# Second feed-forward: first convolution tap on ScalarE, gate product and low half moved one step later

## Chip, cores and metric

The kernel runs on one core of a Trainium2 chip. The metric is the device time of one execution in microseconds. Everything is fp32. The run shown is one profiled execution; the time quoted is a median over unprofiled runs.

## The reference

Two transformer blocks with two layers each run one after the other on an activation of 256 tokens by 1024. The change touches only the feed-forward of the second block, which is computed once in each of its two layers:

```
h = rmsnorm(x, norm_ffn_g[l])
u = centred_depthwise_conv(h @ w_up[l], ffn_conv_w[l])   # w_up: 1024 x 5632, three taps along the tokens
u_gate, u_val = jnp.split(u, 2, axis=-1)                 # 2816 columns each
x = x + (jax.nn.silu(u_gate) * u_val) @ w_down[l]        # w_down: 2816 x 1024
```

`silu(v)` is `v * sigmoid(v)`. The convolution multiplies each column (a feature) at tokens t-1, t and t+1 by three weights of that column and adds.

## The kernel before

**Products in three passes.** Every fp32 matrix product is made of three matmuls (`mm3`, L682 to L684) over operands that are split into a high half (rounded to the type fp32r) and a low half (the rest): high x high, high x low, low x high. Weights come from memory in units of 128 x 2048 numbers into `raw` (5 buffers). ScalarE writes the high half `whi` (L1231), VectorE subtracts it for the low half `wlo` (L1610); both have 3 buffers, so ScalarE's split of unit u waits until TensorE is through with unit u-3. Activations are split in the same way: `high` on ScalarE (key `hiT`), `low` on VectorE (L1617).

**One written order.** `Plan` writes one list of steps. Every engine walks through the same list and issues its own part of each step, in this order: `step` first issues the weight splits up to two units ahead of the step (`ahead`), and then the step's own work (`do`). An engine runs its instructions strictly in this order. A split of weights that stands behind another instruction on its engine thus waits for it.

**The stage.** `ffn2(l)` first runs a normalisation (`rms`) and `fstart` (clears the two border columns of `ci`, loads the convolution weights `cwf`). Then come the up products `("up", l, cb, k)`: column blocks cb = 0 to 5, of 512 columns each (256 in block 5), k = 0 for the gate half and k = 1 for the value half. The result of one has the features on the partitions: 4 chunks of 128 features x 256 tokens (2 in block 5). A full one uses two units of weights, one in block 5 a single unit. Behind them come the down products `("dn", l, 0)` and `("dn", l, 1)`, of six units each, unit j of which needs chunk group j of `hT2`, the hidden activation. So units 0 to 21 are the up weights, and 22 on the down weights; these numbers within the stage are used below. At the last unit of an up product (cb, k), each engine does in `product`:

- ScalarE: the eviction from PSUM to `ci[k]` (L1464), then `convolved` for the product before: for k = 0 the sigmoid of `co[0]` into `sgf` (L1474), which waits for the taps; for k = 1 the high half `hT2h` (L1477), which waits for the last product `co[0] * co[1]` (key `fm`).
- VectorE: `convolve` for the product before: tap 0 (L2421, `co[k] = ci[k] * w0`, one instruction for each chunk), taps 1 and 2 (L2423, multiply and add), and then for k = 0 the gate product `co[0] *= sgf` (L2427), which waits for the sigmoid; for k = 1 `co[1] = co[0] * co[1]` (L2430) and `low` into `hT2l` (L1617), which waits for `hT2h`.

A "turn" is what VectorE does from one `convolve` to the next. The turn of k = 1 or k = 0 is named after the half that it convolves. After the product (5, 1) the order goes on with the first unit of the down product, `fend` (`convolve` and `convolved` of (5, 1)), and the other down units.

Of the kernel before, what the change touches and what calls it, by code (L numbers as in the profile page):

```python
# [12 lines left out]
ACT = mybir.ActivationFunctionType  # L13
# [8 lines left out]
ALL = slice(None)  # L22
# [224 lines left out]
class Plan:  # L247
# [219 lines left out]
    def ffn2(self, l):  # L467
        a, m, o = self.a, self.m, self.order
        o += [("rms", f"f2{l}"), ("fstart", l)]
        xt = [("xT", f"f2{l}", 1)]  # L470
        for cb in range(6):
            for k in range(2):
                o += self.gemm(("up", l, cb, k), "ffn2", m.xT, a["w_up_2"][l], "b", 8, 2816 * k + 512 * cb,
                               min(512, 2816 - 512 * cb), xt)
        need = [("hT2", l, c) for c in range(6)]
        dn = [self.gemm(("dn", l, cb), "ffn2", m.hT2, a["w_down_2"][l], "a", 22, 512 * cb, 512, need) for cb in range(2)]
        o += dn[0][0:1] + [("fend", l)] + dn[0][1:] + dn[1]
        if l == 1:
            o += [("out", "out")]

# [741 lines left out]
class Scalar(Engine):  # L1222
# [157 lines left out]
    def product(self, g, G):  # L1380

        e, m, nm = self.e, self.m, g[0]
        if nm in ("bo", "bd", "wo", "w2", "w3", "e3", "oat", "od", "wo2", "dn"):
            if nm == "w3":
                cb, n = g[1], G.w // 128
                e.wait_ge(*self.at("ev", "w3", cb))
                e.activation(m.hT[0][:, 4 * cb:4 * cb + n, :],
                             m.tmp[:, 0:2 * G.w].rearrange("p (k n) -> p k n", n=256), ACT.Copy) \
                    .then_inc(*self.up("hi_ffn", ("hiT", "hT", cb)))
            return  # L1390
        ps = self.psum(*g)
        if nm == "g":
            return
        e.wait_ge(*self.at("full", *g))
        if nm in ("q", "k"):
            dst = m.qT if nm == "q" else m.kT
            e.activation(dst[:, 4 * g[2]:4 * g[2] + 4, :], bands(ps, 4), ACT.Copy).then_inc(*self.up("a_qkv", ("ev",) + g))
        elif nm == "v":
            e.activation(m.v[:, :, 512 * g[2]:512 * g[2] + 512], bands(ps), ACT.Copy) \
                .then_inc(*self.up("a_qkv", ("ev",) + g))  # L1400
        elif nm in ("cq", "ck"):
            dst = m.cq if nm == "cq" else m.ck
            e.activation(dst[:, :, :], bands(ps)[:, :, 0:G.w], ACT.Copy).then_inc(*self.up("a_latent", ("ev",) + g))
        elif nm == "uq":
            e.activation(m.qr[:, :, G.n0:G.n0 + G.w], bands(ps)[:, :, 0:G.w], ACT.Copy) \
                .then_inc(*self.up("a_latent", ("ev",) + g))
        elif nm == "ukv":
            cb = g[2]
            for t in range(2):
                pv = ps[:, t * 512:t * 512 + 512].rearrange("p (h n) -> p h n", h=4)  # L1410
                e.activation(m.kk[:, t, 4 * cb:4 * cb + 4, 0:64], pv[:, :, 0:64], ACT.Copy)
                ins = e.activation(m.vm[:, t, 4 * cb:4 * cb + 4, :], pv[:, :, 64:128], ACT.Copy)
            ins.then_inc(*self.up("a_latent", ("ev",) + g))
        elif nm == "w1":
            if g[1]:
                e.wait_ge(*self.at("ev", "w3", g[1] - 1))
            e.activation(m.sgm[:, 0:2 * G.w], ps[:, 0:2 * G.w], ACT.Sigmoid).then_inc(*self.up("a_ffn", ("sgm", g[1])))
        elif nm == "pp":
            gP = m.gP if g[1] == 0 else m.gP1
            e.activation(gP[:, g[2]], bands(ps), ACT.Copy).then_inc(*self.up("a_ple", ("ev",) + g))  # L1420
        elif nm == "pg":
            if g[2]:
                e.wait_ge(*self.at("py", g[1], 0))
            gE = m.gE if g[1] == 0 else m.gE1
            e.activation(gE[:, :, :], bands(ps), ACT.Sigmoid).then_inc(*self.up("a_ple", ("ev",) + g))
        elif nm == "rt":
            e.activation(m.lgt[:, :, :], bands(ps)[:, :, 0:8], ACT.Copy).then_inc(*self.up("a_route", ("ev",) + g))
        elif nm == "e1":
            ex, cb = g[1:]
            if cb > 1:  # L1430
                e.wait_ge(*self.at("full", "ac", ex, cb - 2))
            elif ex:
                e.wait_ge(*self.at("full", "sc", ex - 1, cb))
            e.activation(m.hb[:, cb % 2, 0:self.tiles, :], bands(ps)[:, 0:self.tiles, :], ACT.Sigmoid) \
                .then_inc(*self.up("a_moe", ("hbs", ex, cb)))
        elif nm == "e2":
            e.activation(m.hb[:, g[2], 0:self.tiles, :], bands(ps)[:, 0:self.tiles, :], ACT.Copy) \
                .then_inc(*self.up("a_moe", ("ev",) + g))
        elif nm == "dc":
            if g[2] == 2:  # L1440
                e.wait_ge(*self.at("tap", g[1], 0))
            e.activation(m.cin[g[2] % 2][:, :, 2:258], bands(ps, 4), ACT.Copy).then_inc(*self.up("a_conv", ("ev",) + g))
        elif nm == "z":
            zr = m.odn[:, :, :, :].rearrange("p t h n -> p t (h n)")
            for r, t, y in ROWS:
                ins = e.activation(zr[r, y, :], bands(ps)[r, t, :], ACT.Copy)
            ins.then_inc(*self.up("a_conv", ("ev",) + g))
        elif nm == "bd2":
            self.beta(g, ps)
        elif nm == "gm":  # L1450
            e.activation(m.gm[:, (g[2] + 2) % 4], bands(ps), ACT.Sigmoid).then_inc(*self.up("a_gate2", ("ev",) + g))
        elif nm == "qa":
            e.activation(m.qk[:, :, 0:8, :], ps[:, :].rearrange("p (t h n) -> p t h n", t=2, n=64), ACT.Copy) \
                .then_inc(*self.up("a_grid", ("ev",) + g))
        elif nm == "ka":
            pv = ps[:, :].rearrange("p (t h n) -> p t h n", t=2, n=64)
            e.activation(m.qk[:, :, 8:10, :], pv[:, :, 0:2, :], ACT.Copy)
            e.activation(m.va[:, :, :, :], pv[:, :, 2:4, :], ACT.Copy).then_inc(*self.up("a_grid", ("ev",) + g))
        elif nm == "up":
            _, l, cb, k = g  # L1460
            n = G.w // 128
            if cb:
                e.wait_ge(*self.at("ftap", l, cb - 1, k))
            e.activation(m.ci[k][:, 0:n, 1:257], ps[:, 0:2 * G.w].rearrange("p (c n) -> p c n", c=n), ACT.Copy) \  # L1464
                .then_inc(*self.up("a_ffn2", ("ev",) + g))
            if (cb, k) != (0, 0):
                self.convolved(l, cb - 1 + k, 1 - k)

    def convolved(self, l, cb, k):
        e, m = self.e, self.m  # L1470
# [132 lines left out]
class Vector(Engine):  # L1603
# [26 lines left out]
    def do(self, step):  # L1630
# [149 lines left out]
        elif what == "fstart":  # L1780
            for k in range(2):
                e.memset(m.ci[k][:, :, 0:1], 0.0)
                ins = e.memset(m.ci[k][:, :, 257:258], 0.0)
            ins.then_inc(*self.up("d_ffn2"))
        elif what == "fend":
            self.convolve(a[0], 5, 1)

    def tables(self):

# [245 lines left out]
    def product(self, g, G):  # L2035
# [6 lines left out]
        ps = self.psum(*g)  # L2042
        if nm == "up":
            _, l, cb, k = g
            if (cb, k) != (0, 0):
                self.convolve(l, cb - 1 + k, 1 - k)
            return
# [357 lines left out]
        e.tensor_tensor(of, of, m.zs[:, :, :], ALU.mult).then_inc(*self.up("d_delta", ("odn", l)))  # L2405

    def convolve(self, l, cb, k):
        e, m = self.e, self.m
        n = min(512, 2816 - 512 * cb) // 128
        co, ci = m.co[k], m.ci[k]  # L2410
        if (cb, k) == (0, 0):
            e.wait_ge(*self.at("ld", "cwf", l))
        e.wait_ge(*self.at("ev", "up", l, cb, k))
        if cb:
            e.wait_ge(*self.at("hiT", "hT2", l, cb - 1))
        for tap in range(3):
            e.wait_ge(*self.prev)
            for c in range(n):
                wc = m.cwf[:, 22 * k + 4 * cb + c, tap:tap + 1]
                if tap == 0:  # L2420
                    ins = e.tensor_scalar(co[:, c, :], ci[:, c, 0:256], wc, None, ALU.mult)  # L2421
                else:
                    ins = e.scalar_tensor_tensor(co[:, c, :], ci[:, c, tap:tap + 256], wc, co[:, c, :], ALU.mult, ALU.add)  # L2423
            ins.then_inc(*self.up("d_ffn2", ("ftap", l, cb, k)))
        if k == 0:
            e.wait_ge(*self.at("fsg", l, cb))
            e.tensor_tensor(co[:, 0:n, :], co[:, 0:n, :], m.sgf[:, 0:n, :], ALU.mult).then_inc(*self.up("d_ffn2"))  # L2427
        else:
            e.wait_ge(*self.prev)
            e.tensor_tensor(co[:, 0:n, :], m.co[0][:, 0:n, :], co[:, 0:n, :], ALU.mult) \  # L2430
                .then_inc(*self.up("d_ffn2", ("fm", l, cb)))
            self.low("ffn2", ("hT2", l, cb), co[:, 0:n, :], m.hT2, (ALL, slice(4 * cb, 4 * cb + n), ALL))


class Pool(Engine):
# [299 lines left out]
```

## Time and profile before

| | |
|---|---|
| median of 3 runs | 3000.89 us (2997.72 to 3003.07) |
| the profiled execution | 3003.25 us |
| its span, first to last instruction | 3001.4 us |
| mean granted TensorE clock | 0.967 of full speed |
| TensorE matmul busy | 2781.7 us, 93% of the span |
| VectorE busy | 2140.1 us, 71% |
| ScalarE busy | 1597.6 us, 53% |
| GpSimd busy | 141.8 us, 5% |

Busy shares are over the whole span. The stage in question runs twice, from about 2276 to 2489 us and from about 2789 us to the end. Matmuls are pipelined, so that TensorE counts as busy for longer than a matmul holds up the next.

### The profile page before, as it was taken

To read this page: it belongs to the slowest core of one execution; us is meant where nothing else is said; L and a number is where in the kernel's file an instruction comes from. 1 tells how busy PE (TensorE), PEld (TensorE's weight loads), DVE (VectorE), ACT (ScalarE), POOL (GpSimd) and SP (SyncE) were. 2 spreads that over 40 slices of the span, in tenths; PEclk is the share of its full clock that TensorE was granted. 3 is DMA by queue.
4 is the path that set the end of the run, shared out by engine and by line. 5 is a ranking of instruction groups with operands and counts; after the bars stand their busy time and mean duration, and the time that the engine had idled before them with its cause. 6 is when DMAs were issued, how large, how long until landed. Compare 5 with 4: busy or idle time off the path is not lost.

```text
span 3001.4 us, 44783 instructions
## 1 busy us (share of the span) xinstructions
PE 2781.7 (93%) x19184; PEld 2363.0 (79%) x19184; DVE 2140.1 (71%) x2148; ACT 1597.6 (53%) x1532; POOL 141.8 (5%) x154
## 2 busy tenths in 40 slices
PE   7988999998889999999999999979989989988998
PEld 7867799886777787878778787768778978877896
DVE  4557655646659897988889898867755866766685
ACT  3345443354437676767667676736544434654442
POOL 0000000000000000000000000000420000051000
PEclk9899999999989999999999999989999999999999
DMA  5253555455348898999989999953214544312452
GB/s 182 96 153 133 179 177 182 134 169 145 117 150 311 317 354 318 342 327 346 326 316 343 329 353 334 350 166 114 72 66 142 169 166 151 124 59 93 142 169 98
DMA packets 360206, 616.16 MB, mean 205 GB/s; under 512 B 13760, under 2 KB 117056, under 8 KB 359984
## 3 DMA queue, kind: packets, MB, share of 16 engines
q1 hardware_dynamic: 354784, 597.50, 57.6%
q0 software_dynamic: 5200, 15.47, 2.1%
q8 instruction: 168, 2.75, 0.4%
q14 instruction: 54, 0.44, 0.0%
HBM read 611.88 MB, written 1.05 MB: 204 GB/s over the span
## 4 chain that ended last, share of the span: by engine, by line
PE 74%; DVE 15%; ACT 6%; issue 4%; DMA 1%; POOL 0%; ACTq 0%; DVEq 0%; SPq 0%; POOLq 0%
PE ps L682 21%; PE ps L684 21%; PE ps L683 21%; DVE wlo L1610 4%; ACT whi L1231 3%; DVE co L2423 2%; PE ps L914 1%; PE ps L945 1%; PE ps L1091 1%; PE ps L935 1%; DVE cv L2240 1%; PE ps L1070 1%; DVE co L2421 1%; PE ps L775 1%; PE ps L1102 1%
## 5 line engine op out<-in xcount | busy, mean ns | idle before, releaser
L1610 DVE TENSOR_TENSOR wlo<-raw,whi 128x2048 fp32r<-128x2048 f32 (+2 forms) x588 | 1303.5, 2223 | 460.3 <-ACT whi L1231 455.9
L1231 ACT ACTIVATE whi<-raw 128x2048 fp32r<-128x2048 f32 (+2 forms) x588 | 1090.6, 1859 | 463.3 <-PE ps L684 450.6
L682 PE MATMUL ps<-whi,xTh 128*128 128x512 f32 (+5 forms) x1488 | 599.8, 403 | 30.3 <-issue 16.8
L683 PE MATMUL ps<-wlo,xTh 128*128 128x512 f32 (+5 forms) x1488 | 588.7, 396 | 0.0
L684 PE MATMUL ps<-whi,xTl 128*128 128x512 f32 (+5 forms) x1488 | 587.7, 395 | 0.0
L682 PE MATMUL ps<-xTh,whi 128*128 128x256 f32 x1504 | 428.8, 285 | 24.1 <-DVE xTl L1617 11.9
L684 PE MATMUL ps<-xTh,wlo 128*128 128x256 f32 x1504 | 427.2, 284 | 0.0
L683 PE MATMUL ps<-xTl,whi 128*128 128x256 f32 x1504 | 425.7, 283 | 0.0
L682 PEld LDWEIGHTS ps<-whi,xTh 128*128 128x128 f32 x1488 | 291.4, 196 | 96.6 <-issue 21.2
L684 PEld LDWEIGHTS ps<-whi,xTl 128*128 128x128 f32 x1488 | 291.8, 196 | 63.9
L683 PEld LDWEIGHTS ps<-wlo,xTh 128*128 128x128 f32 x1488 | 292.4, 196 | 58.7
L682 PEld LDWEIGHTS ps<-xTh,whi 128*128 128x128 f32 x1504 | 286.1, 190 | 27.8 <-issue 15.4
L683 PEld LDWEIGHTS ps<-xTl,whi 128*128 128x128 f32 x1504 | 286.9, 191 | 0.1
L684 PEld LDWEIGHTS ps<-xTh,wlo 128*128 128x128 f32 x1504 | 284.8, 189 | 0.0
L682 PE MATMUL ps<-whi,hTeh 128*128 128x512 f32 x448 | 178.3, 398 | 0.0
L683 PE MATMUL ps<-wlo,hTeh 128*128 128x512 f32 x448 | 177.6, 396 | 0.0
L684 PE MATMUL ps<-whi,hTel 128*128 128x512 f32 x448 | 177.6, 396 | 0.0
L684 PEld LDWEIGHTS ps<-whi,hTel 128*128 128x128 f32 x448 | 84.4, 188 | 20.6
L682 PEld LDWEIGHTS ps<-whi,hTeh 128*128 128x128 f32 x448 | 84.4, 188 | 20.2
L683 PEld LDWEIGHTS ps<-wlo,hTeh 128*128 128x128 f32 x448 | 84.4, 188 | 20.1
L682 PE MATMUL ps<-whi,hT2h 128*128 128x512 f32 x176 | 71.4, 406 | 14.7 <-DVE wlo L1610 14.4
L2423 DVE SCALAR_TENSOR_TENSOR co<-ci,cwf,co 128x256 f32<-128x256 f32 x176 | 74.0, 481 | 1.7
(533 smaller groups left out, 3450.2 us busy)
## 6 DMA issues: line engine op xcount, KB each, us to landing
raw<-in_expert_w_dram SPq DMA_DIRECT2D x336, 1024.0 KB, 6.0
raw<-in_w_in_dram SPq DMA_DIRECT2D x76, 1024.0 KB, 5.1
raw<-in_w_up_dram SPq DMA_DIRECT2D x44, 1024.0 KB, 5.3
raw<-in_dense_w_dram SPq DMA_DIRECT2D x32, 1024.0 KB, 5.1
raw<-in_w_down_dram SPq DMA_DIRECT2D x20, 1024.0 KB, 5.9
raw<-in_w_out_dram SPq DMA_DIRECT2D x16, 1024.0 KB, 5.1
raw<-in_w_branch_diff_dram SPq DMA_DIRECT2D x8, 1024.0 KB, 5.0
raw<-in_w_ple_gate_dram SPq DMA_DIRECT2D x8, 1024.0 KB, 5.1
```

The costliest lines, as they stand in the source:

```text
L682: self.e.matmul(out, ah, bh, start=start, stop=False)
L683: self.e.matmul(out, ah, bl, start=False, stop=False)
L684: return self.e.matmul(out, al, bh, start=False, stop=stop)
L775: ins = self.e.transpose(ps[:, k * 128:k * 128 + 128], src[:, t, k * 128:k * 128 + 128], self.m.ident[:, :])
L914: ins = e.matmul(ps[:, d * 256:d * 256 + 256], m.xs[half][:, q, (d0 + d) * 128:(d0 + d + 1) * 128], m.sel[:, q, :], start=(q == 0), stop=( ...
L935: ins = e.transpose(ps[:, o:o + 128], m.hb[:, cb % 2, t, k * 128:k * 128 + 128], m.ident[:, :])
L945: ins = e.matmul(ps[:, q * 512:q * 512 + 512], m.selgT[:, s, q * 128:q * 128 + 128], m.hb[:, cb, s, :], start=(s == 0), stop=(s == self.ti ...
L1070: ins = self.e.transpose(out(r_), src[:, 128 * r_:128 * r_ + 128], self.m.ident[:, :])
L1091: ins = e.matmul(ps[half(a_), span(512 * c + 64 * r_)], m.E[d][r, s], TT[r, s], start=True, stop=True)
L1231: self.e.activation(self.m.hi[u % NHL][:, 0:n], self.m.raw[u % NRAW][:, 0:n], ACT.Copy) \
L1610: self.e.tensor_tensor(self.m.lo[u % NHL][:, 0:n], self.m.raw[u % NRAW][:, 0:n], self.m.hi[u % NHL][:, 0:n].bitcast(F32), ALU.subtract) \
L2423: ins = e.scalar_tensor_tensor(co[:, c, :], ci[:, c, tap:tap + 256], wc, co[:, c, :], ALU.mult, ALU.add)
```

## The change

The first tap of the convolution moves from VectorE to ScalarE. There it stands in `product`, behind the eviction and behind `convolved`, as one activation (copy with a scale for each partition) for each chunk. It is tap 0 of the product just evicted, not of the product before. ScalarE waits there for its own eviction, for `cwf` and the cleared borders at the first product, and for `low` of the block before, where it writes `co[1]`.

On VectorE `convolve` keeps taps 1 and 2. The gate product moves from the end of the k = 0 turn to the k = 1 turn, behind its taps and ahead of the last product. The low half moves out of `convolve` into `hidden_low`, which runs at the start of the next k = 0 turn; for block 5 it is a step of its own, `flast`, behind the second down unit.

```diff
-        o += dn[0][0:1] + [("fend", l)] + dn[0][1:] + dn[1]
+        o += dn[0][0:1] + [("fend", l)] + dn[0][1:2] + [("flast", l)] + dn[0][2:] + dn[1]
...
             e.activation(m.ci[k][:, 0:n, 1:257], ps[:, 0:2 * G.w].rearrange("p (c n) -> p c n", c=n), ACT.Copy) \
                 .then_inc(*self.up("a_ffn2", ("ev",) + g))
-            if (cb, k) != (0, 0):
+            copied = self.prev
+            if (cb, k) == (0, 0):
+                e.wait_ge(*self.at("ld", "cwf", l))
+                e.wait_ge(*self.at("fzero", l))
+            else:
                 self.convolved(l, cb - 1 + k, 1 - k)
+            e.wait_ge(*copied)
+            if cb and k:
+                e.wait_ge(*self.at("hT2", l, cb - 1))
+            for c in range(n):
+                wc = m.cwf[:, 22 * k + 4 * cb + c, 0:1]
+                ins = e.activation(m.co[k][:, c, :], m.ci[k][:, c, 0:256], ACT.Copy, scale=wc)
+            ins.then_inc(*self.up("a_ffn2", ("tap0", l, cb, k)))
...
+        elif what == "flast":
+            self.hidden_low(a[0], 5)
...
             _, l, cb, k = g
+            if cb and k:
+                self.hidden_low(l, cb - 1)
             if (cb, k) != (0, 0):
                 self.convolve(l, cb - 1 + k, 1 - k)
...
-        e.wait_ge(*self.at("ev", "up", l, cb, k))
-        if cb:
-            e.wait_ge(*self.at("hiT", "hT2", l, cb - 1))
-        for tap in range(3):
-            e.wait_ge(*self.prev)
+        e.wait_ge(*self.at("tap0", l, cb, k))
+        for tap in (1, 2):
+            if tap == 2:
+                e.wait_ge(*self.prev)
             for c in range(n):
                 wc = m.cwf[:, 22 * k + 4 * cb + c, tap:tap + 1]
-                if tap == 0:
-                    ins = e.tensor_scalar(co[:, c, :], ci[:, c, 0:256], wc, None, ALU.mult)
-                else:
-                    ins = e.scalar_tensor_tensor(co[:, c, :], ci[:, c, tap:tap + 256], wc, co[:, c, :], ALU.mult, ALU.add)
+                ins = e.scalar_tensor_tensor(co[:, c, :], ci[:, c, tap:tap + 256], wc, co[:, c, :], ALU.mult, ALU.add)
             ins.then_inc(*self.up("d_ffn2", ("ftap", l, cb, k)))
-        if k == 0:
+        if k == 1:
+            done = self.prev
             e.wait_ge(*self.at("fsg", l, cb))
-            e.tensor_tensor(co[:, 0:n, :], co[:, 0:n, :], m.sgf[:, 0:n, :], ALU.mult).then_inc(*self.up("d_ffn2"))
-        else:
+            e.tensor_tensor(m.co[0][:, 0:n, :], m.co[0][:, 0:n, :], m.sgf[:, 0:n, :], ALU.mult).then_inc(*self.up("d_ffn2"))
+            e.wait_ge(*done)
             e.wait_ge(*self.prev)
             e.tensor_tensor(co[:, 0:n, :], m.co[0][:, 0:n, :], co[:, 0:n, :], ALU.mult) \
                 .then_inc(*self.up("d_ffn2", ("fm", l, cb)))
-            self.low("ffn2", ("hT2", l, cb), co[:, 0:n, :], m.hT2, (ALL, slice(4 * cb, 4 * cb + n), ALL))
+
+    def hidden_low(self, l, cb):
+        n = min(512, 2816 - 512 * cb) // 128
+        self.low("ffn2", ("hT2", l, cb), self.m.co[1][:, 0:n, :], self.m.hT2, (ALL, slice(4 * cb, 4 * cb + n), ALL))
```

## Rows read from the trace of the kernel before

**Rows 1.** The page, part 1: busy time of each engine, share of span

```profile
PE 2781.7 (93%) x19184; PEld 2363.0 (79%) x19184; DVE 2140.1 (71%) x2148; ACT 1597.6 (53%) x1532; POOL 141.8 (5%) x154
```

**Rows 2.** TensorE waits, 2270 to 2440 us: line, releaser, total, times, longest

```profile
PE ps L682 <- DVE wlo L1610: 8.6, 5, 5.1
```

**Rows 3.** The same view, 2785 to 3001 us, second layer

```profile
PE ps L682 <- DVE wlo L1610: 10.7, 6, 5.1
```

**Rows 4.** Busy time by stretch: length, engines (instructions), granted clock, DMA share, GB/s

```profile
2294.00:2341.22 47.22, 47.22 (x396) 47.22 (x395) 36.17 (x49) 24.09 (x17) 0.00 (x0) 1.00 0.51 161
...
2366.28:2391.34 25.06, 23.51 (x194) 23.16 (x194) 21.47 (x33) 11.27 (x8) 0.00 (x0) 1.00 0.50 165
```

**Rows 5.** VectorE in order of time: start, us, instruction, idle before it and releaser

```profile
2366.20 1.14 DVE L2421 TENSOR_SCALAR co<-ci,cwf 128x256 f32<-128x256 f32 x4
2367.37 3.38 DVE L2423 SCALAR_TENSOR_TENSOR co<-ci,cwf,co 128x256 f32<-128x256 f32 x8
2370.79 1.23 DVE L2430 TENSOR_TENSOR co<-co,co 128x1024 f32<-128x1024 f32 x1
2373.14 1.23 DVE L1617 TENSOR_TENSOR hT2l<-co,hT2h 128x1024 fp32r<-128x1024 f32 x1 [1.13 <-ACT hT2h L1477]
2374.94 4.50 DVE L1610 TENSOR_TENSOR wlo<-raw,whi 128x2048 fp32r<-128x2048 f32 x2 [0.58 <-ACT whi L1231]
2379.36 1.14 DVE L2421 TENSOR_SCALAR co<-ci,cwf 128x256 f32<-128x256 f32 x4
2380.53 3.38 DVE L2423 SCALAR_TENSOR_TENSOR co<-ci,cwf,co 128x256 f32<-128x256 f32 x8
2385.04 1.23 DVE L2427 TENSOR_TENSOR co<-co,sgf 128x1024 f32<-128x1024 f32 x1 [1.13 <-ACT sgf L1474]
2386.85 4.49 DVE L1610 TENSOR_TENSOR wlo<-raw,whi 128x2048 fp32r<-128x2048 f32 x2 [0.58 <-ACT whi L1231]
2391.26 1.14 DVE L2421 TENSOR_SCALAR co<-ci,cwf 128x256 f32<-128x256 f32 x4
```

**Rows 6.** ScalarE in the same stretch, in order of time

```profile
2372.05 1.06 ACT L1477 ACTIVATE hT2h<-co 128x1024 fp32r<-128x1024 f32 x1 [6.91 <-DVE co L2430]
2373.01 3.70 ACT L1231 ACTIVATE whi<-raw 128x2048 fp32r<-128x2048 f32 x2
2376.62 1.00 ACT L1464 ACTIVATE ci<-ps 128x1024 f32<-128x1024 f32 x1
2383.95 1.06 ACT L1474 ACTIVATE sgf<-co 128x1024 f32<-128x1024 f32 x1 [6.33 <-DVE co L2423]
2384.91 3.71 ACT L1231 ACTIVATE whi<-raw 128x2048 fp32r<-128x2048 f32 x2
```

**Rows 7.** ScalarE groups by shape: busy us, mean ns | idle before, releaser

```profile
L1504 ACT ACTIVATE sg__147<-sg__147,mxg 128x256 f32<-128x256 f32 x32 | 15.9, 499 | 17.2 <-DVE mxg L1909 17.2
```

**Rows 8.** VectorE at the start of the first layer's stage

```profile
2304.19 1.14 DVE L2421 TENSOR_SCALAR co<-ci,cwf 128x256 f32<-128x256 f32 x4
...
2311.67 4.49 DVE L1610 TENSOR_TENSOR wlo<-raw,whi 128x2048 fp32r<-128x2048 f32 x2 [0.58 <-ACT whi L1231]
```

**Rows 9.** ScalarE at the start of the first layer's stage

```profile
2306.77 1.28 ACT L1474 ACT_TABLE_LOAD   x1
2308.77 1.06 ACT L1474 ACTIVATE sgf<-co 128x1024 f32<-128x1024 f32 x1 [0.71 <-DVE co L2423]
```

**Rows 10.** VectorE's weight splits at the end of the first layer's stage

```profile
2411.91 2.29 DVE L1610 TENSOR_TENSOR wlo<-raw,whi 128x2048 fp32r<-128x2048 f32 x1 [0.58 <-ACT whi L1231]
...
2422.85 2.29 DVE L1610 TENSOR_TENSOR wlo<-raw,whi 128x2048 fp32r<-128x2048 f32 x1 [0.57 <-ACT whi L1231]
...
2430.00 2.29 DVE L1610 TENSOR_TENSOR wlo<-raw,whi 128x2048 fp32r<-128x2048 f32 x1 [1.11 <-ACT whi L1231]
...
2437.88 5.63 DVE L1610 TENSOR_TENSOR wlo<-raw,whi 128x2048 fp32r<-128x2048 f32 x3 [1.11 <-ACT whi L1231]
```

**Rows 11.** TensorE in a short stretch: busy time and granted clock

```profile
2426.00:2429.00 3.00, 3.00 (x9) 0.55 0.89 281
```

More of the change, by code:

```diff
@@ L1783, in do @@
                 ins = e.memset(m.ci[k][:, :, 257:258], 0.0)
-            ins.then_inc(*self.up("d_ffn2"))
+            ins.then_inc(*self.up("d_ffn2", ("fzero", a[0])))
         elif what == "fend":
             self.convolve(a[0], 5, 1)
+        elif what == "flast":
+            self.hidden_low(a[0], 5)
     def tables(self):
```

## The prediction

> **What bounds the kernel now.** I read the page first. TensorE is busy for 93% of the span, VectorE 71%, ScalarE 53% [rows 1]. An average over unlike stages says nothing of this one, so I went to TensorE's waits inside the stage: it waits for VectorE's split `wlo`, 8.6 us in 5 waits in the first layer and 10.7 us in 6 in the second [rows 2, 3]. So VectorE's side is the slower one, but not by much. The stretches show from when: from 2294 to 2341 us TensorE is busy throughout (47.22 of 47.22 us, 396 matmuls, so 0.119 us each), and a block of 192 matmuls would take it 22.9 us. From 2366.28 to 2391.34 us one block takes 25.06 us [rows 4]. The head start is used up by then, and about 2.2 us a block are lost.
>
> What makes 25.06 us is a loop through two engines, and VectorE's and ScalarE's timelines show it link by link [rows 5, 6]. I measure each link from start to start, as neighbours overlap a little.
>
> Turn k=1: tap 0 1.17 (2366.20 to 2367.37), taps 1 and 2 3.42, `co0*co1` 1.26 (2370.79 to ScalarE's 2372.05), `hT2h` 0.96, first `whi` 1.93, two `wlo` 4.42: 13.16 us. Turn k=0: tap 0 1.17, taps 3.42, sigmoid 0.96, `whi` 1.94, two `wlo` 4.41: 11.90 us. The two are 25.06 us.
>
> Two things do not appear in these sums: the gate product of turn k=0 (2385.04) and the low half of turn k=1 (2373.14). Both run while VectorE waits for ScalarE's `whi` anyway: of the 2.9 us between the last tap or product and the next `wlo`, VectorE idles 1.13 + 0.58 and works 1.23 at no cost. They are free today. And `whi` cannot come sooner, since in ScalarE's written order it stands behind `hT2h` or the sigmoid.
>
> **The change, part by part.**
>
> *Tap 0 leaves VectorE.* Saves 1.17 us in every turn, on the loop.
>
> *Tap 0 on ScalarE.* It stands behind the sigmoid or `hT2h` and ahead of the next `whi`, for which VectorE, and then TensorE, wait. ScalarE's idle 6.3 and 6.9 us [rows 6] lie before these instructions and are no cover: the order puts the taps behind them. So all of it is on the loop. No row has this form. The nearest is ScalarE's activation of 128x256 in SBUF with a bias for each partition, 0.50 us [rows 7]; neighbours overlap by 0.10 (`hT2h` takes 1.06 and the next starts after 0.96), so 0.40 each and 1.60 for four. From below: a plain copy takes 1.06 for 1024 columns and about 1.90 for 2048 [rows 6], so 0.43 for 256 by that line, 0.33 spaced, 1.32 for four. From above: 0.50 without overlap, 2.00. I take 0.40, because the scale is an operand for each partition as the bias in that row is.
>
> *Gate product into turn k=1.* It leaves the free place and comes between the taps and `co0*co1`, on which it bears: +1.26 in turn k=1, the spacing of such a product and what waits for it; 0 saved in turn k=0.
>
> *Low half into turn k=0.* It leaves the other free place and stands ahead of the taps: +1.15 (1.23 less the 0.08 by which neighbours overlap, as 4.50 against 4.42). Nothing saved in turn k=1.
>
> So turn k=1: 13.16 - 1.17 + 1.26 + 1.60 = 14.85, +1.69. Turn k=0: 11.90 - 1.17 + 1.15 + 1.60 = 13.48, +1.58. A block goes from 25.06 to 28.33 us, and VectorE's idle time in it from 3.6 to about 9 us. That is the point: VectorE gets less work and more waiting.
>
> *The waits.* The added ones (own eviction, `cwf`, the borders, `low` of the block before) are met long before, save the own eviction at the very first product, behind which ScalarE's split has slack. TensorE's buffers bring no new wait: two units need 11.5 us in a turn of 13.5.
>
> *The start.* The loop governs from the `wlo` at 2311.67 on [rows 8]. After the change two tap passes run from 2304.19 to 2307.61, but the sigmoid also waits for its table load, which ends at 2308.05 [rows 9]. From there 0.96 + 1.60 + 1.94 give 2312.6: +0.9.
>
> *Full turns.* From 2311.67 to 2411.91 [rows 8, 10] are 100.24 us, four blocks of 25.06. Added: 4 x (1.69 + 1.58) = 13.1.
>
> *The end.* Three shorter turns follow, to 2422.85, 2430.00 and 2437.88 [rows 10], where a tap 0 issued for block 5 has two chunks (0.80). Value half of block 4: -1.17 + 1.26 + 0.80 = +0.9. Gate half of block 5: -0.6 + 1.15 + 0.80 = +1.35. Value half of block 5, with nothing for ScalarE behind it: -0.6 + 0.7 = +0.1. `flast` stands behind the split at 2437.88, for which TensorE waits, and its result is wanted two units later: 0. SyncE's loads wait for `wlo` five units back and get more time; GpSimd's load of the next gains waits for `flast` and has until the next normalisation at about 2484.
>
> Per layer 0.9 + 13.1 + 2.35 = 16.35. Behind 2437.88 TensorE alone sets the time, so all of it reaches the end. The second layer has the same pattern and waits [rows 3]: in all 32.7 us. On the profiled execution's 3003.25 us that is 3036. This execution lies 2.4 us above the median of 3000.89; against the median I forecast 3033.6 us.
>
> **A rule that speaks the other way.** VectorE is the busiest engine beside TensorE in the block, 21.47 of 25.06 us, with ScalarE at 11.27 [rows 4]. The Trainium skill says, in Perfetto Trace Analysis, "Identifying Performance Opportunities", that work on the most contended engine is what to improve, and under "Optimizing Scalar/DVE Operations" that handing work from a saturated VectorE to ScalarE may make sense. By that rule the change should gain; by the loop it loses, because VectorE idles for ScalarE in each turn. It is the first rival.
>
> **The rivals.**
>
> *Faster, VectorE's work is the bound.* Its instructions alone are, after the change, 8.83 + 2 x 3.42 + 3 x 1.23 = 19.4 us a block, under TensorE's 22.9. If the two engines overlapped freely, the stage would run at TensorE's pace and all of its waits would go, 19.3 us: 2982 us. For it speaks the busy share. Against it: ScalarE's part that VectorE has to sit out would have to be under 22.9 - 19.4 = 3.5 us a block, and it is 5.8 us now and 9 then. 4%.
>
> *No change: the taps on ScalarE are hidden.* If they ran in ScalarE's idle time ahead of the sigmoid, the turns would change by +0.09 and -0.02 and the whole by under 2 us: 3001 to 3003. The written order speaks against it. 4%.
>
> *Cheaper taps*, 0.33 each: in a layer 40 tap instructions are on the loop (four blocks of 8, two at each of two short turns, four at the start), so 5.6 us less: 3028. 18%. *Dearer taps*, 0.50: 8 us more: 3042. 7%.
>
> *A table load.* The first sigmoid of the stage costs a load of 1.28 us [rows 9], and the copies behind it none. If a copy with a scale needed another table, each k=0 turn would carry one load between sigmoid and taps, some 11 in all: +14, 3048. 4%.
>
> *TensorE's clock.* Behind its longest wait, 5.1 us, the granted clock was 0.55, near the lower of the levels 1.2 and 2.4 GHz [rows 2, 11]. After the change TensorE idles 2.7 us in the mean turn. A turn needs 11.46 us at full clock out of 14.2, so below a mean clock of 0.81 TensorE would become the bound; at 0.70 it needs 16.4, and some 16 full turns give +35: 3069. The waits of today's turns left the clock at 1.00 [rows 4]. 3%. The Trainium skill has the rule in TensorE: Matmul & The Clock Gate, "HAM oscillation": a TensorE that keeps idling between bursts falls back. By it the sum could be this one; but slower work fills the gap itself.
>
> **How the numbers follow.** My sum holds with 60%. Range 3026 to 3042 us: from the cheap taps with 2 us for the spread of runs to the dear ones. 0.2% of this time, 6 us, is about what can be told from no change. Slower by more: 0.92; within it 0.04; faster 0.04.
>
> **What the profile after would show.** Right: a block of about 28.3 us in full turns; ScalarE groups of four activations of 128x256 at 0.50 us, start to start 0.40, between sigmoid or `hT2h` and `whi`; the idle before `wlo` for `whi` grown from 0.58 to about 4.5 in turn k=1; VectorE's busy time lower by 88 x 0.29, some 25 us; TensorE's waits for `wlo` up by over 25 us; everything outside the stage as before. Wrong: a block at 22.9 to 25 us; `whi` ahead of the taps; table loads between; a granted clock under 0.9 in full turns.

## The result, and the profile after

The changed kernel takes 3027.9 us (median of 4 runs, 3023.41 to 3033.41) against 2999.3 us (4 runs) before: a ratio of 1.0098, 95% interval 1.0077 to 1.0120. It is 1% slower, about 29 us, where the forecast was 33 us over the 3000.89 us known then. Its time lies inside the range of 3026 to 3042 us, 2 us above the lower end. The profiled execution took 3030.98 us with a span of 3029.2 us, 27.8 us longer than before.

The page's busy times of the changed kernel:

```profile
PE 2792.0 (92%) x19184; PEld 2372.8 (78%) x19184; DVE 2112.9 (70%) x2060; ACT 1631.6 (54%) x1620; POOL 141.8 (5%) x154
```

VectorE is busy for 27 us less and ScalarE for 34 us more than in [rows 1]. TensorE executes the same matmuls and is busy with them for 10 us longer. TensorE's waits for the weight split, in the two layers (2270 to 2460 us, 2800 to 3030 us):

```profile
PE ps L682 <- DVE wlo L1621: 22.1, 10, 5.9
```

```profile
PE ps L682 <- DVE wlo L1621: 22.0, 10, 6.0
```

Before, the second layer has 10.7 us [rows 3]. The 8.6 us of [rows 2] are short of one wait, because that window ends at 2440 us, inside the stage. To 2460 us the first layer of the kernel before has the same as the second:

```profile
PE ps L682 <- DVE wlo L1610: 10.7, 6, 5.1
```

So the waits have grown from 21.4 to 44.1 us in all. A block of full turns on the two engines, in order of time (it is the one before that of [rows 5, 6]; the blocks from 2311.73 us on are alike to 0.1 us). VectorE:

```profile
2339.97 4.50 DVE L1621 TENSOR_TENSOR wlo<-raw,whi 128x2048 fp32r<-128x2048 f32 x2 [4.53 <-ACT whi L1231]
2344.38 3.38 DVE L2435 SCALAR_TENSOR_TENSOR co<-ci,cwf,co 128x256 f32<-128x256 f32 x8
2347.68 1.22 DVE L2440 TENSOR_TENSOR co<-co,sgf 128x1024 f32<-128x1024 f32 x1
2349.00 1.23 DVE L2443 TENSOR_TENSOR co<-co,co 128x1024 f32<-128x1024 f32 x1
2354.76 4.49 DVE L1621 TENSOR_TENSOR wlo<-raw,whi 128x2048 fp32r<-128x2048 f32 x2 [4.53 <-ACT whi L1231]
2359.16 1.22 DVE L1628 TENSOR_TENSOR hT2l<-co,hT2h 128x1024 fp32r<-128x1024 f32 x1
2360.30 3.38 DVE L2435 SCALAR_TENSOR_TENSOR co<-ci,cwf,co 128x256 f32<-128x256 f32 x8
2368.21 4.49 DVE L1621 TENSOR_TENSOR wlo<-raw,whi 128x2048 fp32r<-128x2048 f32 x2 [4.53 <-ACT whi L1231]
```

ScalarE:

```profile
2350.26 1.06 ACT L1488 ACTIVATE hT2h<-co 128x1024 fp32r<-128x1024 f32 x1 [7.62 <-DVE co L2443]
2351.22 1.69 ACT L1477 ACTIVATE co<-ci,cwf 128x256 f32<-128x256 f32 x4
2352.82 3.69 ACT L1231 ACTIVATE whi<-raw 128x2048 fp32r<-128x2048 f32 x2
...
2363.71 1.06 ACT L1485 ACTIVATE sgf<-co 128x1024 f32<-128x1024 f32 x1 [6.28 <-DVE co L2435]
2364.68 1.69 ACT L1477 ACTIVATE co<-ci,cwf 128x256 f32<-128x256 f32 x4
2366.28 3.70 ACT L1231 ACTIVATE whi<-raw 128x2048 fp32r<-128x2048 f32 x2
```

From split to split (2339.97 to 2368.21) the block is 28.24 us; it was 25.06. VectorE now waits 4.53 us for `whi` in each turn. ScalarE shows why: the four taps (1.69 us busy; `whi` starts 1.60 us after the first of them) stand between the high half or the sigmoid and `whi`, and the gate product (2347.68) and the low half (2359.16) no longer lie in the wait. TensorE by stretch (length, busy time and matmuls, granted clock, DMA share, GB/s), two blocks and a piece near the end of the stage:

```profile
2339.97:2368.21 28.24, 23.50 (x195) 1.00 0.46 150
2368.21:2396.44 28.23, 23.50 (x182) 0.94 0.45 149
...
2439.00:2442.00 3.00, 3.00 (x8) 0.50 0.65 195
```

Start and end of the first layer's stage, which answer to [rows 8 to 10]. ScalarE and then VectorE:

```profile
2293.37 1.03 ACT L1464 ACTIVATE ci<-ps 128x1024 f32<-128x1024 f32 x1 [3.78 <-PE ps L684]
...
2305.94 1.28 ACT L1485 ACT_TABLE_LOAD   x1
2307.23 1.06 ACT L1485 ACTIVATE sgf<-co 128x1024 f32<-128x1024 f32 x1
```

```profile
2311.73 4.50 DVE L1621 TENSOR_TENSOR wlo<-raw,whi 128x2048 fp32r<-128x2048 f32 x2 [5.00 <-ACT whi L1231]
...
2424.67 2.29 DVE L1621 TENSOR_TENSOR wlo<-raw,whi 128x2048 fp32r<-128x2048 f32 x1 [4.53 <-ACT whi L1231]
...
2436.44 2.29 DVE L1621 TENSOR_TENSOR wlo<-raw,whi 128x2048 fp32r<-128x2048 f32 x1 [3.72 <-ACT whi L1231]
...
2444.87 2.29 DVE L1621 TENSOR_TENSOR wlo<-raw,whi 128x2048 fp32r<-128x2048 f32 x1 [3.29 <-ACT whi L1231]
...
2452.77 2.29 DVE L1621 TENSOR_TENSOR wlo<-raw,whi 128x2048 fp32r<-128x2048 f32 x1 [2.50 <-ACT whi L1231]
```

For what follows I use, beside the medians, a measure that leaves out what happens elsewhere in the kernel: the length of the stage in one trace. It runs from ScalarE's first eviction (L1464) to its first instruction of the next normalisation (first layer) or to the end of the span (second layer). Before it is 184.5 and 194.8 us, after 200.2 and 210.5 us: 15.7 us longer each time. TensorE in the first layer's stage, before and after:

```profile
2294.21:2478.72 184.51, 173.50 (x1197) 0.99 0.51 168
```

```profile
2293.37:2493.61 200.24, 178.05 (x1197) 0.97 0.47 155
```

Of the 15.7 us it is idle for 11.2; for the other 4.5 it is busy longer with the same 1197 matmuls, at a lower mean clock. Each length is rounded to 0.1 us, so differences are good to about 0.1 us a layer. The first eviction, ahead of which no kernel here differs, came anywhere from 2287.0 to 2299.6 us in the twelve traces, so differences of a few us between spans mean nothing.

### The profile page after: what moved, and what is told of

Its sections match the earlier page's. It is cut to its first block, busy times and chain, and to the rows that moved or that the text cites. A ratio compares the mean times of both kernels' runs of the same rounds, so it can differ in the third digit from the quotient of the medians.

```text
span 3029.2 us, 44785 instructions
## 1 busy us (share of the span) xinstructions
PE 2792.0 (92%) x19184; PEld 2372.8 (78%) x19184; DVE 2112.9 (70%) x2060; ACT 1631.6 (54%) x1620; POOL 141.8 (5%) x154
## 4 chain that ended last, share of the span: by engine, by line
PE 74%; DVE 15%; ACT 7%; issue 4%; DMA 1%; POOL 0%; DVEq 0%; ACTq 0%; SPq 0%; POOLq 0%
PE ps L682 21%; PE ps L684 21%; PE ps L683 21%; DVE wlo L1621 4%; ACT whi L1231 3%; DVE co L2435 2%; PE ps L914 1%; ACT co L1477 1%; PE ps L945 1%; PE ps L1091 1%; PE ps L935 1%; DVE cv L2255 1%; PE ps L1070 1%; PE ps L1102 1%; PE ps L775 1%
## 5 line engine op out<-in xcount | busy, mean ns | idle before, releaser
L682 PE MATMUL ps<-xTh,whi 128*128 128x256 f32 x1504 | 434.3, 289 | 44.1 <-DVE wlo L1621 27.6
```

Of the source, the lines that this page charges most:

```text
L682: self.e.matmul(out, ah, bh, start=start, stop=False)
```

## Experiments

| kernel | ratio to before (95%) | stage, both layers, against before | TensorE waits for `wlo` |
|---|---|---|---|
| before | | | 10.7, 10.7 us |
| the change | 1.0098 (1.0077 to 1.0120) | +31.4 us | 22.1, 22.0 |
| places_only | 1.0066 (1.0046 to 1.0086) | +26.5 | 18.6, 18.5 |
| taps_only | 1.0029 (1.0013 to 1.0045) | +6.6 | 11.7, 11.8 |
| fixed_scale | 1.0078 (1.0054 to 1.0102) | +25.5 | 17.5, 17.4 |
| taps_early | 1.0004 (0.9988 to 1.0019) | +2.9 | 11.3, 11.4 |
| taps_early_places_back | 0.9913 (0.9894 to 0.9931) | -21.6 | 2.9, 2.9 |
| change_split_first | 0.9926 (0.9909 to 0.9942) | -22.5 | 2.7, 2.7 |
| change_split_first_b | 0.9912 (0.9892 to 0.9933) | -22.6 | 2.7, 2.7 |
| before_split_first | 0.9950 (0.9932 to 0.9968) | -13.7 | 4.5, 4.7 |
| before_split_first_b | 0.9948 (0.9929 to 0.9966) | -13.8 | 4.7, 4.6 |
| early_and_split_first | 0.9926 (0.9908 to 0.9944) | -23.6 | 2.1, 2.1 |

Each ratio is to runs of the kernel before that were made together with it. The diffs are excerpts, against the changed kernel where nothing else is said.

**The change's two halves apart.** places_only keeps all three taps on VectorE and moves only the gate product and the low half:

```diff
-            for c in range(n):
-                wc = m.cwf[:, 22 * k + 4 * cb + c, 0:1]
-                ins = e.activation(m.co[k][:, c, :], m.ci[k][:, c, 0:256], ACT.Copy, scale=wc)
...
-        for tap in (1, 2):
...
+        for tap in range(3):
...
+                if tap == 0:
+                    ins = e.tensor_scalar(co[:, c, :], ci[:, c, 0:256], wc, None, ALU.mult)
```

> Only the gate product and the low half are moved; tap 0 stays on VectorE. If both stood in VectorE's idle place at no cost and now stand on the loop: turn k=1 13.16 + 1.26 = 14.4 us, turn k=0 11.90 + 1.15 = 13.05 us, a block 27.5 us; four blocks 9.6 us and the short turns 1.26 + 1.15 + 0.7 = 3.1 us a layer, in all +25 us over before. Rival, that moving them is free and the whole loss comes from the taps on ScalarE: a block of 25.1 us and no change.

taps_only moves only tap 0:

```diff
-        if k == 1:
-            done = self.prev
+        if k == 0:
             e.wait_ge(*self.at("fsg", l, cb))
...
+            self.hidden_low(l, cb)
```

> Only tap 0 moves to ScalarE, in the place that the change gives it; the gate product and the low half stand where they were. If four taps of 0.40 us on the loop replace 1.17 us there: turns of 13.6 and 12.3 us, a block of 25.9 us, +3.5 us a layer, +7 us over before; with places_only this adds up to the whole change. Rival, VectorE's work as the bound: VectorE has 1.17 us less in each turn, a block falls towards 22.9 us, -15 us or so. Rival, that the loss is all from the taps: +28 us.

VectorE in places_only:

```profile
2347.66 4.49 DVE L1610 TENSOR_TENSOR wlo<-raw,whi 128x2048 fp32r<-128x2048 f32 x2 [2.93 <-ACT whi L1231]
2352.07 1.22 DVE L1617 TENSOR_TENSOR hT2l<-co,hT2h 128x1024 fp32r<-128x1024 f32 x1
2353.40 1.14 DVE L2424 TENSOR_SCALAR co<-ci,cwf 128x256 f32<-128x256 f32 x4
...
2360.89 4.49 DVE L1610 TENSOR_TENSOR wlo<-raw,whi 128x2048 fp32r<-128x2048 f32 x2 [2.93 <-ACT whi L1231]
```

The turn of k=0 is 13.23 us (2347.66 to 2360.89). VectorE's wait of 2.93 us is as long as the 1.13 + 0.58 us of waiting and 1.23 us of work in its place before; it is only no longer filled. The expectation had 13.05 us for the turn; tap 0 starts 1.33 us behind the low half, because in this kernel it waits for it, not 1.14 us as in the change. VectorE in taps_only:

```profile
2346.84 4.49 DVE L1621 TENSOR_TENSOR wlo<-raw,whi 128x2048 fp32r<-128x2048 f32 x2 [2.18 <-ACT whi L1231]
...
2355.75 1.23 DVE L2435 TENSOR_TENSOR co<-co,sgf 128x1024 f32<-128x1024 f32 x1 [1.13 <-ACT sgf L1485]
2359.15 4.50 DVE L1621 TENSOR_TENSOR wlo<-raw,whi 128x2048 fp32r<-128x2048 f32 x2 [2.17 <-ACT whi L1231]
```

Turn k=0 there is 12.31 us (12.3 expected): the product is back in the wait. With 26.5 and 6.6 us against 25 and 7 expected, the halves add up to 33.1 us where the whole change has 31.4. The extra 0.19 us by which tap 0 waits for the low half in places_only would explain it: five turns in each of two layers make 1.9 us. So four fifths of the loss are the two instructions that left their free places, and one fifth is tap 0, dearer on ScalarE's side of the loop (1.60) than it was on VectorE's (1.17). Both rivals, the moved places free or VectorE's work the bound, fall.

**The price of a tap.** In fixed_scale tap 0 is multiplied by a constant, so its result is not the reference's.

```diff
-                wc = m.cwf[:, 22 * k + 4 * cb + c, 0:1]
-                ins = e.activation(m.co[k][:, c, :], m.ci[k][:, c, 0:256], ACT.Copy, scale=wc)
+                ins = e.activation(m.co[k][:, c, :], m.ci[k][:, c, 0:256], ACT.Copy, scale=0.5)
```

> The change with the taps on ScalarE scaled by a constant instead of by the weight of each partition, so tap 0 is not the reference's. If the operand for each partition makes 0.07 us of each 0.40: the four taps start 0.33 us apart, a block is 27.7 us instead of 28.24, and the whole 5 to 6 us faster than the change. If the operand costs nothing: 28.24 us and the change's time.

ScalarE:

```profile
2353.51 1.06 ACT L1487 ACTIVATE hT2h<-co 128x1024 fp32r<-128x1024 f32 x1 [7.61 <-DVE co L2442]
2354.48 1.32 ACT L1476 ACTIVATE co<-ci 128x256 f32<-128x256 f32 x4
2355.71 3.69 ACT L1231 ACTIVATE whi<-raw 128x2048 fp32r<-128x2048 f32 x2
```

`whi` starts 1.23 us after the first tap, against 1.60 (2351.22 to 2352.82) in the change. The operand for each partition makes 0.09 us of each tap's 0.40; the plain one takes 0.31. That is a little less than the 0.33 us expected, and the block is 27.48 us (27.7 expected). The stages are 5.9 us shorter in all than those of the change. The ratios (1.0078 and 1.0098) point the same way, but their intervals overlap.

**The place of the taps.** taps_early gives `co` a second pair of buffers (by the parity of cb), so that the taps may run right behind the eviction, ahead of the sigmoid or the high half:

```diff
-            else:
-                self.convolved(l, cb - 1 + k, 1 - k)
             e.wait_ge(*copied)
-            if cb and k:
-                e.wait_ge(*self.at("hT2", l, cb - 1))
+            if cb > 1:
+                e.wait_ge(*self.at(*(("hT2", l, cb - 2) if k else ("fm", l, cb - 2))))
...
+            if (cb, k) != (0, 0):
+                self.convolved(l, cb - 1 + k, 1 - k)
```

> The change with the four taps ahead of the sigmoid or the high half on ScalarE, into a second pair of buffers, so that they run in ScalarE's idle time. The gate product and the low half stay moved. If only the place of the taps makes them cost: turns of 13.25 and 11.9 us, a block of 25.1 us, 3001 us, no difference from before. If the taps cost wherever they stand: 3028 us.

taps_early_places_back also puts the product and the low half back, as taps_only does.

> As taps_early, but with the gate product and the low half back in VectorE's idle places. The loop then has 1.17 us less in each turn and nothing more: 12.0 and 10.7 us, a block of 22.7 us, just under TensorE's 22.9: TensorE sets the pace but for the short turns, about 2984 us. Rival, that VectorE's idle time is not made by the order: 3001 us or more.

ScalarE in taps_early:

```profile
2357.14 1.72 ACT L1475 ACTIVATE co<-ci,cwf 128x256 f32<-128x256 f32 x4
2363.39 1.06 ACT L1485 ACTIVATE sgf<-co 128x1024 f32<-128x1024 f32 x1 [4.54 <-DVE co L2435]
2364.36 3.71 ACT L1231 ACTIVATE whi<-raw 128x2048 fp32r<-128x2048 f32 x2
```

The same four taps of 1.71 us now run at 2357.14, in ScalarE's idle time, which still leaves 4.54 us before the sigmoid, and `whi` follows 0.97 us after the sigmoid starts. The loss is gone (1.0004), though VectorE's instructions are those of the change. Of the 31.4 us in the stage 2.9 are left, 2.1 of them at its two starts, where the taps stand ahead of the table load. The second pair of buffers lets the taps move and is not what gains: in the change they follow the high half by 0.96 us with no wait for a buffer. So a tap costs by where it stands, and the 1.17 us a turn taken off VectorE are spent again by the two instructions that left the wait. With them back in it, VectorE:

```profile
2346.14 4.49 DVE L1621 TENSOR_TENSOR wlo<-raw,whi 128x2048 fp32r<-128x2048 f32 x2 [0.58 <-ACT whi L1231]
...
2355.06 1.23 DVE L2435 TENSOR_TENSOR co<-co,sgf 128x1024 f32<-128x1024 f32 x1 [1.13 <-ACT sgf L1485]
2356.86 4.50 DVE L1621 TENSOR_TENSOR wlo<-raw,whi 128x2048 fp32r<-128x2048 f32 x2 [0.58 <-ACT whi L1231]
```

A turn k=0 of 10.72 us (10.7 expected), TensorE's waits down to 2.9 us a layer, and 0.9% faster than before: what the offload is worth when its taps lie in idle time and the two other instructions stay in theirs.

**The order on ScalarE.** change_split_first is the change with one line more, before_split_first the kernel before with the same line: ScalarE issues its next weight split behind the eviction.

```diff
             copied = self.prev
+            self.more()
```

> The change, but ScalarE issues its next weight split right behind the eviction, ahead of the sigmoid or the high half and of the taps. The unit that frees its buffer is the one that the eviction waited for. If the loss is VectorE waiting for a split that stands behind the taps: VectorE's idle time before it goes, its work of 19.4 us a block is under TensorE's 22.9, and the stage runs at TensorE's pace, 2981 to 2985 us, 0.5 to 0.6% under before. If the taps slow something else (ScalarE's work, memory ports): no change from the change, 3028 us.

> The kernel before with the same early split on ScalarE and nothing else. VectorE then waits only for the sigmoid or the high half inside a turn: turns of about 12.5 and 11.2 us, a block of 23.75 us against TensorE's 22.9. Over four blocks 5.2 us and over the short turns about 3 us a layer less, most of TensorE's waits: 2984 us, some 0.5% under before and within 4 us of the changed kernel with the early split. If the moved places matter once the split is early, that kernel is more than 4 us ahead.

VectorE in change_split_first:

```profile
2361.71 2.28 DVE L1622 TENSOR_TENSOR wlo<-raw,whi 128x2048 fp32r<-128x2048 f32 x1
2366.32 2.29 DVE L1622 TENSOR_TENSOR wlo<-raw,whi 128x2048 fp32r<-128x2048 f32 x1 [2.33 <-ACT whi L1231]
```

The first split starts with no wait behind VectorE's taps (2361.71). VectorE now waits 2.33 us only for the second one, which on ScalarE still stands behind tap 0. So the loop is shorter, not gone. VectorE's block is 23.83 us (from the split at 2337.88 to the one at 2361.71), still above the 23.04 us that TensorE takes when it does not wait: two turns of 11.52 us from eviction to eviction (2298.51, 2310.03, 2321.55). The difference, 0.8 us a block, comes off the head start that TensorE's weights have at the start of the stage, and four blocks do not use it up: the evictions stay 11.52 us apart until 2390.67. The expectation, that VectorE's waiting goes and only its work of 19.4 us a block counts, was wrong on this, though nearly right on the time (2981 to 2985 us). The change with this line is 0.7 to 0.9% faster than before. So the place of both splits behind the sigmoid or high half and the taps is what turned less VectorE work into more time. The line alone, on the kernel before, brings 0.5%, as expected (2993.19 us beside a before of 3005.03): that kernel had the loop too, and a block of it is now 23.71 us (23.75 expected). The two kernels with the early split had intervals that overlapped a little, so both ran again together, with a third that joins the early taps, the old places and the early split:

> The change with the early split once more, beside before_split_first_b on the same chip, since each differed from before by much the same. TensorE's waits for the split were 2.7 us a layer in its trace and 4.5 in the other: if nothing else differs, it is about 4 us (0.1%) ahead of before_split_first_b. If the change is worth more once the split is early: 8 us or more.

> The kernel before with the early split, as the partner of change_split_first_b: 0.5% under before, 2985 to 2990 us.

> Taps early on ScalarE, gate product and low half in their old places, and the split early as well. Without the early split TensorE waits 2.9 us a layer, so both together can give no more than 6 us over it: 2975 to 2982 us, the pace of TensorE. If the early split costs something of its own, it is above that.

2973.12 us (2969.52 to 2980.96) against 2986.79 us (2980.66 to 2989.68): the change is worth 14 us by the medians and 8.8 us by the stages once the split is early, more than the 4 us of TensorE's waits that I had expected. In the first layer both reach the last eviction alike (121.3 and 121.8 us after the first); the difference, 51.9 against 55.9 us, lies behind it, in the short turns (VectorE's first one takes 8.57 us against 10.27). There before_split_first has the longest wait, 4.2 us, and half the clock behind it. TensorE in before_split_first and then in change_split_first, in the short turns of each:

```profile
2421.00:2424.00 3.00, 0.00 (x0) 0.99 0.00 0
...
2427.00:2430.00 3.00, 3.00 (x9) 0.50 0.80 309
```

```profile
2426.00:2429.00 3.00, 3.00 (x14) 1.00 0.79 264
...
2432.00:2435.00 3.00, 1.68 (x7) 1.00 0.17 27
```

The whole piece behind the last eviction, in before_split_first_b and then in change_split_first_b, takes the 4.0 us apart:

```profile
2416.51:2472.45 55.94, 52.03 (x213) 0.94 0.56 188
```

```profile
2408.36:2460.27 51.91, 49.84 (x213) 1.00 0.60 203
```

TensorE is idle 1.8 us longer there (3.9 against 2.1), which is the longer wait, and busy 2.2 us longer with the same 213 matmuls at the lower clock.

The third kernel, at 0.9926 and 2978.11 us, is no better than the best of the others. Its stage is the shortest of all by 1 us, and VectorE's turns in it are 11.52 us each, those of TensorE: its pace is reached, as expected, but for 2.1 us of waits a layer.

## Why the prediction was right, point by point

*The loop.* Right, link by link: blocks of 28.24 us against 28.33 forecast, turns (from split to split) of 14.79 and 13.45 against 14.85 and 13.48. It is shown from two sides: taps_early takes the taps out of the loop, change_split_first takes one of the two splits from behind them, and in each the loss goes.

*Tap 0 on ScalarE.* Right: 1.60 us for four from the first tap to `whi`. The choice of the row with an operand for each partition over the plain line was the right one. fixed_scale shows the plain price, 1.23 us, where that line gave 1.32.

*Gate product and low half.* 1.26 and 1.15 us forecast. The low half took 1.14 (2359.16 to 2360.30). The product took 1.32 to the one that waits for it, but itself starts 3.30 us after the first instruction of the tap passes, not 3.42, as it does not wait for them: 1.20 net.

*Start, full turns, end.* All three as forecast or a little less. Start: from the first eviction to the split at 2311.73 18.36 us, against 17.46 before: +0.9, as forecast. Full turns: 112.94 against 100.24 us, +12.7 (13.1 forecast). End: 28.10 against 25.97, +2.1 (2.35 forecast). A layer is 15.7 us longer, not 16.35, 0.4 us less in the full turns (the product alone has 0.06 in each block) and 0.2 us in the short ones. From the last of these splits to the next normalisation the first layer takes 40.84 us before and after, as the prediction said: there TensorE alone sets the time.

*The whole.* 31.4 us in the stage against 32.7. The span grew by only 27.8, because the rest of this trace was 3.6 us shorter, within the scatter told above. The medians are 28.6 us apart. So what was forecast well is the stage; that the median also came out within 5 us has the scatter of the rest in it.

*TensorE's clock.* The rival named a real thing that did not decide. TensorE idled about 2.4 us in the mean turn (28.24 less 23.50, halved), more exactly 3.0 and 1.7 us in alternate turns. The granted clock was 1.00 in the block from 2339.97 and 0.94 in the next two; behind the longest wait of the stage it was 0.50, the level of 1.2 GHz. In the block from 2368.21 it fell about 1 us after the end of a wait of 3.0 us, and stayed down for about 3 us:

```profile
2386.00:2387.00 1.00, 1.00 (x9) 0.66 0.61 75
2387.00:2388.00 1.00, 1.00 (x6) 0.50 1.03 355
```

Yet the block at 0.94 is as long as the one at 1.00 (28.23 and 28.24 us): the slower work fills a part of the wait for the split.

*The signs.* TensorE's waits were to rise by over 25 us and rose by 22.7. This sign failed, and the prediction's 8.6 us for the first layer is the reading of the short window told above; it enters the sum of the time nowhere. What the waits fell short by is in the 4.5 us a layer for which TensorE worked longer. VectorE's busy time fell by 27 us, not 25. The taps are 0.49 us each and 0.40 from start to start (0.50 and 0.40 forecast). No table load stands between them, and the clock in full turns stayed above 0.9.

*The first rival* failed as a forecast: VectorE's work was not the bound. Its price, 2982 us, is what the kernel takes when the loop is short enough (2973 to 2980 us came out, 0.7 to 0.9% faster than before). It subtracted 19.3 us of waits; with the first layer read in full they are 21.4. Its condition was that VectorE sits out less than 3.5 us a block. change_split_first reached TensorE's pace with twice 2.33 us, by the head start, which the condition left out.

## What to carry to other kernels

Before moving work off the busiest engine, find out whether that engine is short of time or waits in a loop through another one. In a loop, what counts is where an instruction stands: one that fills a wait is free, and moving it out of the wait costs its whole length, while a move to the idle engine saves nothing if it lands ahead of what the first engine waits for. The cheapest repair here was one line: on ScalarE, issue the instruction that VectorE waits for ahead of those that wait themselves. It gave 0.5% on the kernel before, and 0.7 to 0.9% together with the change.

## What the runs showed of the hardware

A ScalarE activation of 128x256 from SBUF to SBUF starts the next 0.31 us later with a constant scale and 0.40 us later with one for each partition, 0.09 us for the operand (1.23 and 1.60 us for four). The Trainium skill has this in ScalarE: Activation LUTs, "What ACT_TABLE_LOAD costs", which gives about 93 ns for such an operand; the runs agree. TensorE with waits of 3.0 and 1.7 us in alternate turns kept its full clock in one block and had a mean of 0.94 in the next, where it ran at 0.50 for about 3 us behind a wait of 3.0 us; both blocks took the same time, 28.24 and 28.23 us, in one and the same trace.
